# A mixture-of-experts tail on one Trainium2 core: the last expert's rows are placed by one-hot products on TensorE, and the other experts' rows are gathered and summed inside the round loop

## The reference

```python
top_v, top_i = lax.top_k(logits, TOP_K)          # TOP_K = 2 of N_EXPERTS = 8
gates = jax.nn.softmax(top_v, axis=-1)
combine = jnp.sum(jax.nn.one_hot(top_i, N_EXPERTS) * gates[..., None], axis=-2)
out = jnp.zeros_like(hn)
for e in range(N_EXPERTS):
    out = out + combine[..., e:e + 1] * swiglu(hn, w_gu[e], w_down[e])   # D_FF_EXPERT = 1024
return h + out
```

## Time and profile before

| | before |
|---|---|
| median of 3 runs | 1511.39 us (1510.7, 1511.39, 1518.9) |
| the profiled execution's own time | 1512.38 us |
| its span | 1510.7 us |
| PE busy | 1421.7 us (94%) |
| DVE busy | 898.5 us (59%) |
| ACT busy | 640.0 us (42%) |
| POOL busy | 241.2 us (16%) |

### The profile page before, as it was taken

How to read it: one execution, slowest core, us unless ns; L and a number is a source line. 1 busy time by engine, 2 the same in 40 slices (tenths; PEclk the granted TensorE clock), 3 DMA queues, 4 the chain that set the end, 5 groups by cost and what they waited for, 6 DMA issues and landing times. The chain is left out here.

```text
span 1510.7 us, 31344 instructions
## 1 busy us (share of the span) xinstructions
PE 1421.7 (94%) x12965; PEld 1263.5 (84%) x12965; DVE 898.5 (59%) x1201; ACT 640.0 (42%) x1077; POOL 241.2 (16%) x243
## 2 busy tenths in 40 slices
PE   6999999999899999999999998879799999999993
PEld 6999988888699999999999998549667777777772
DVE  5677635765755444434444666553467777777775
ACT  4344535442333223222323432563555656565561
POOL 0111016765120000000111101340042000000002
PEclk8999999999999999999999999799889999999997
DMA  6677422000433333332333522005269888888886
GB/s 186 222 280 265 135 66 63 2 2 30 151 116 84 97 98 83 85 109 58 96 91 116 168 57 91 1 1 150 76 210 303 297 279 296 292 276 285 272 286 219
DMA packets 170203, 226.48 MB, mean 150 GB/s; under 512 B 11545, under 2 KB 135090, under 8 KB 170010
## 3 DMA queue, kind: packets, MB, share of 16 engines
q1 hardware_dynamic: 160246, 191.44, 40.6%
q0 software_dynamic: 8976, 30.88, 5.8%
q10 hardware_dynamic: 862, 2.50, 0.5%
HBM read 188.78 MB, written 38.28 MB: 150 GB/s over the span
## 5 line engine op out<-in xcount | busy, mean ns | idle before, releaser
L281 DVE TENSOR_TENSOR w_lo<-w_raw,w_hi 128x2048 fp32r<-128x2048 f32 (+1 forms) x70 | 151.6, 2171 | 95.8 <-ACT w_hi L273 95.8
L226 PE MATMUL P<-xf_hi,w_hi 128*128 128x260 f32 x704 | 199.0, 283 | 2.0 <-DVEq L1857 1.2
L226 PE MATMUL P<-xf_hi,w_lo 128*128 128x260 f32 x704 | 198.9, 283 | 0.0
L226 PE MATMUL P<-xf_lo,w_hi 128*128 128x260 f32 x704 | 198.2, 282 | 0.0
L273 ACT ACTIVATE w_hi<-w_raw 128x2048 fp32r<-128x2048 f32 (+1 forms) x71 | 128.1, 1810 | 126.6 <-PE P L226 114.5
L226 PE MATMUL P<-xa_hi,w_hi 128*128 128x260 f32 x512 | 145.4, 284 | 5.0 <-DVE xa_lo L324 5.0
L226 PE MATMUL P<-xa_hi,w_lo 128*128 128x260 f32 x512 | 145.2, 284 | 0.0
L226 PE MATMUL P<-xa_lo,w_hi 128*128 128x260 f32 x512 | 144.8, 283 | 0.0
L226 PEld LDWEIGHTS P<-xf_hi,w_hi 128*128 128x128 f32 x704 | 132.5, 188 | 2.6 <-issue 1.4
L226 PEld LDWEIGHTS P<-xf_hi,w_lo 128*128 128x128 f32 x704 | 132.4, 188 | 0.0
L226 PEld LDWEIGHTS P<-xf_lo,w_hi 128*128 128x128 f32 x704 | 132.4, 188 | 0.0
(11 more groups left out here) (569 smaller groups left out, 3420.4 us busy)
## 6 DMA issues: line engine op xcount, KB each, us to landing
raw_more_moe<-in_moe_w_gu_dram SPq DMA_DIRECT2D x64, 512.0 KB, 5.3
w_raw<-in_moe_w_gu_dram SPq DMA_DIRECT2D x64, 512.0 KB
w_raw<-in_dense_w_gu_dram SPq DMA_DIRECT2D x44, 512.0 KB, 5.0
expert_out<-zeros POOLq DMA_DIRECT2D x40, 512.0 KB, 4.1
w_raw<-in_a_w_in_dram SPq DMA_DIRECT2D x32, 512.0 KB, 5.0
raw_more_moe<-in_moe_w_down_dram SPq DMA_DIRECT2D x32, 512.0 KB, 4.5
w_raw<-in_moe_w_down_dram SPq DMA_DIRECT2D x32, 512.0 KB
w_raw<-in_dense_w_down_dram SPq DMA_DIRECT2D x16, 384.0 KB, 4.0
```

What stands on the lines that cost most here:

```text
L226: ins = nc.tensor.matmul(out[:, b], w, x[:, b * HALF:(b + 1) * HALF], start=(first and n == 0), stop=(last and n == 2))
L281: ins = nc.vector.tensor_tensor(lo, raw, hi.bitcast(F32), ALU.subtract)
```

## The change

Expert 7's results are no longer stored to DRAM. TensorE's last two chunks are ordered by PSUM bank (`last_pair`), so that the over slots and the first half are complete early; ScalarE and VectorE split the results into high and low parts in SBUF (the over slots in a block-diagonal layout, which is cleared by two memsets first). TensorE then multiplies them by one-hot matrices (`spread_base`, `spread_over`), whose columns are tokens, so that PSUM holds expert 7's rows at the tokens' places: eight products of 128x512 per block of tokens, 40 in all. The one-hot matrices are made from expert 7's slot numbers, which GpSimd writes to a small DRAM table and reads back to all partitions, behind `read_table` and ahead of the gathers of tokens for experts 2 to 7. `hi_row` is now the highest slot among experts 0 to 6, `lo_row` the other one; both gathers read stored rows of experts 0 to 6 only (a near row whose expert is 7 has weight zero). The near gathers wait for experts 0 to 5, the far ones for expert 6. The gate weights are worked out in the loop in gate(3), the one-hots in gate(2), the near rows are added in down(6), and the far rows and the placed rows are added and stored at the end of the round. What follows the loop in the kernel before (the twelve small instructions and both additions) is gone.

```diff
+    spread_base, spread_over = flat_pick(1), flat_pick(0)
...
+    last_y_hi, last_y_lo = (xg[part][1].rearrange("p k s -> p (k s)") for part in range(2))
...
     wide = lambda bank: c.P[:, bank:bank + 2]
...
-                store_y(NE - 1)
-                for done, n in ((y_stored[0], 320), (y_stored[1], 240), (y_last, 80)):
+                for n, rows in blocks:
+                    sp.wait_ge(summed, r * NB + (n + 1))
+                    sp.sem_inc(passed, 1)
+                    to = io["y_prompt"][0, n * 128:(n + 1) * 128] if n < NCH else io["y_sample"].rearrange("b s d -> (b s) d")
+                    sp.dma_start(to, L.h_tok[0:rows, n]).then_inc(stored, 16)
+                for done, n in ((y_stored[0], 320), (y_stored[1], 240), (stored, 16 * NB)):
                     sp.wait_ge(done, r * n + n)
                     sp.sem_inc(passed, 1)
                 load_bound(sp, bound)
-            for n, rows in blocks:
-                sp.wait_ge(out_ready, n + 1)
-                to = io["y_prompt"][0, n * 128:(n + 1) * 128] if n < NCH else io["y_sample"].rearrange("b s d -> (b s) d")
-                sp.dma_start(to, L.h_tok[0:rows, n]).then_inc(stored, 16)
...
+                pool.wait_ge(rel_now, r + 1)
+                pool.sem_inc(passed, 1)
+                pool.dma_start(rel_table.rearrange("o (n p) -> p (o n)", p=128), rel[:, :, NE - 1],
+                               allow_slow_non_contiguous=True).then_inc(rel_out, 16)
+                pool.wait_ge(rel_out, r * 16 + 16)
+                pool.sem_inc(passed, 1)
+                pool.dma_start(rel_rows, rel_table.broadcast_to([128, NB * 128])).then_inc(rel_in, 16)
                 for e in range(2, NE):
...
-                for done, n in ((y_stored[0], 320), (y_stored[1], 240)):
-                    pool.wait_ge(done, r * n + n)
+                for done, n, past_ones in ((y_stored[0], 320, 240), (y_stored[1], 240, 240)):
+                    pool.wait_ge(done, r * n + past_ones)
                     pool.sem_inc(passed, 1)
                 for n, rows in blocks:
                     gather_y(near[n], L.lo_row, n, rows, near_in)
-                pool.wait_ge(y_last, r * 80 + 80)
+                pool.wait_ge(y_stored[0], r * 320 + 320)
                 pool.sem_inc(passed, 1)
                 for n, rows in blocks:
                     gather_y(far[n], L.hi_row, n, rows, far_in[n])
...
+                def last_pair(bank, over, hi, lo, fo):
+
+                    pair = (KT - 2, KT - 1)
+                    for t in pair:
+                        m = w.at["down", NE - 1, t]
+                        pe.wait_ge(w.lo_done, r * w.n + (m + 1))
+                        for b in range(4):
+                            ins = pe.matmul(c.P[b * OVER:(b + 1) * OVER, over, 0:256], fo[:, t % 2, t // 2 * OVER:(t // 2 + 1) * OVER],
+                                            w.raw[m % 8][:, b * 256:(b + 1) * 256], start=False, stop=(t == KT - 1))
+                    ins.then_inc(last_over, 1)
+                    for b in range(2):
...
+                            w_hi, w_lo = w.hi[m % 6], w.lo[m % 6]
+                            for a, x in ((hi, w_hi), (hi, w_lo), (lo, w_hi)):
...
+                        if b == 0:
+                            ins.then_inc(last_bank, 1)
...
+                def place_over(n, rows):
+
+                    for b in range(2):
+                        at = slice(b * 512, (b + 1) * 512)
+                        for y, done in ((last_over_hi, over_hi_done), (last_over_lo, over_lo_done)):
+                            if n == 0:
+                                pe.wait_ge(done, r * 4 + 4)
+                            pe.matmul(c.P[0:rows, place_bank[n] + b], spread_over[:, n * 128:n * 128 + rows], y[:, at],
+                                      start=(y is last_over_hi), stop=False)
+
+                def place_base(n, rows):
+
+                    for b in range(2):
+                        at = slice(b * 512, (b + 1) * 512)
+                        for y, done in ((last_y_hi, last_hi), (last_y_lo, last_lo)):
+                            if n == 0:
+                                pe.wait_ge(done, r * 2 + (b + 1))
+                            ins = pe.matmul(c.P[0:rows, place_bank[n] + b], spread_base[:, n * 128:n * 128 + rows], y[:, at],
+                                            start=False, stop=(y is last_y_lo))
...
-                    for _ in down(NE - 1, p, 2, 6, xg_hi[0], xg_lo[0], L.xo[:, 0].rearrange("p k s -> p (k s)")
-                                  .rearrange("p (u s) -> p u s", u=2)):
+                last = (2, 6, xg_hi[0], xg_lo[0], L.xo[:, 0].rearrange("p k s -> p (k s)").rearrange("p (u s) -> p u s", u=2))
+                for p in range(3):
+                    for _ in down(NE - 1, p, *last):
                         pass
-                pe.wait_ge(y_act, r * NE + (NE - 1))
+                last_pair(*last)
...
+                pe.wait_ge(y_act, r * (NE - 1) + (NE - 1))
+                pe.wait_ge(y_dve, r * (NE - 1) + (NE - 1))
+                pe.wait_ge(spread_done, r + 1)
                 pe.sem_inc(passed, 1)
+                place_over(0, 128)
+                place_over(1, 128)
+                place_base(0, 128)
+                place_base(1, 128)
+                for n in range(2, NB):
+                    if n == NCH:
+                        pe.wait_ge(summed, r * NB + 1)
+                        pe.sem_inc(passed, 1)
+                    place_over(n, blocks[n][1])
+                    place_base(n, blocks[n][1])
                 index(0, 5, r * 2 + 3)
                 load_bound(pe, bound)
...
-                        if e < NE - 1:
-                            nc.scalar.activation(y_rows[e % 2][:, 0:512], c.P[:, 4], ACT.Copy).then_inc(y_act, 1)
-                        else:
-                            nc.scalar.activation(flat2(y_rows[e % 2][:, 0:D]), wide(2), ACT.Copy)
-                            nc.scalar.activation(y_rows[e % 2][:, D:D + 256], c.P[:, 6, 0:256], ACT.Copy).then_inc(y_act, 1)
+                        nc.scalar.activation(y_rows[e % 2][:, 0:512], c.P[:, 4], ACT.Copy).then_inc(y_act, 1)
+                    if kind == "down" and q == KT - 1 and e == NE - 1:
+                        act.wait_ge(over_cleared, r + 1)
+                        act.wait_ge(last_over, r + 1)
+                        for b in range(4):
...
+                        act.wait_ge(last_bank, r + 1)
+                        nc.scalar.activation(last_y_hi[:, 0:512], c.P[:, 2], ACT.Copy).then_inc(last_hi, 1)
...
             pick(0)
-            stt(kept, chosen, -float(FAR), slots, ALU.mult, ALU.add)
-            reduce(lo_slot, kept, ALU.min)
-            reduce(hi_slot, tmp, ALU.max)
+            tt(kept, chosen, slots, ALU.mult)
+            reduce(lo_slot, kept, ALU.add)
+            reduce(hi_slot, tmp[:, :, 0:NE - 1], ALU.max)
...
+                def gates():
+
+                    count = 0
+                    def step(ins):
+                        nonlocal count
+                        count += 1
+                        ins.then_inc(gate_step, 1)
+                        dve.wait_ge(gate_step, r * GATE_STEPS + count)
+                    two_in = lambda to, a, b, op: step(nc.vector.tensor_tensor(to, a, b, op))
+                    dve.wait_ge(g_exp, 1)
+                    step(nc.vector.tensor_scalar(m1, g2, 1.0, None, ALU.add))
+                    step(nc.vector.reciprocal(m1, m1))
...
+                    step(nc.vector.tensor_reduce(g_hi, cand, AX, ALU.add))
+                    step(nc.vector.tensor_scalar(is_last, left, 1.0, None, ALU.is_equal))
+                    step(nc.vector.tensor_scalar(g_lo, g_lo, is_last, None, ALU.mult))
+                    step(nc.vector.tensor_scalar(g_hi, g_hi, is_last, None, ALU.mult))
+                    assert count == GATE_STEPS
...
+                def spread():
+
+                    dve.wait_ge(rel_in, r * 16 + 16)
+                    nc.vector.tensor_scalar(spread_base, rel_rows[:, 0:NT], cols(c, CTOK, 1), None, ALU.is_equal)
+                    nc.vector.tensor_scalar(spread_over, rel_rows[:, 0:NT], cols(c, COVER, 1), None, ALU.is_equal)\
+                        .then_inc(spread_done, 1)
+
+                def add_near(n, rows):
+
+                    if n == 0:
+                        dve.wait_ge(near_in, r * (16 * NB) + 16 * NB)
+                    nc.vector.scalar_tensor_tensor(L.h_tok[0:rows, n], near[n][0:rows], g_lo[0:rows, n:n + 1], L.h_tok[0:rows, n],
+                                                   ALU.mult, ALU.add).then_inc(near_added, 1)
+
+                def add_far(n, rows):
+
+                    dve.wait_ge(far_in[n], r * 16 + 16)
+                    dve.wait_ge(near_added, r * NB + (n + 1))
+                    nc.vector.scalar_tensor_tensor(L.h_tok[0:rows, n], far[n], g_hi[0:rows, n:n + 1], L.h_tok[0:rows, n],
+                                                   ALU.mult, ALU.add).then_inc(far_added, 1)
+
```

(44 more changed lines are left out.)

83 lines of the change are left out of this document (50 added, 33 removed).

## The result

The changed kernel takes 1521.36 us (median of 20 runs, 1516.5 to 1526.8) against 1514.39 us for the kernel before (20 runs, 1510.7 to 1523.1): ratio 1.0040, 95% interval 1.0025 to 1.0054. It is slower by 4 to 8 us, where 1.7 us less was forecast and 1515 was the upper end. Of the 11.7 us between the forecast of 1509.7 and 1521.36, 3.0 are the kernel before itself: its median is 1514.39 in 20 runs, and the forecast was made against 1511.39 in three. The profiled execution has a span of 1518.6 us (own time 1520.45), 7.9 us more than the one before.

What follows compares the result with a forecast made beforehand. Experts' stage bound by TensorE, weight stream close behind; tail by a DRAM round trip. Tail gain 4.65 less charges 2.95 gives 1.7 us, taken off the median 1511.39: 1509.7 us; range 1504.5 to 1515, the forecast's own 1507 to 1512.

Steps and rivals of the forecast that it cites:

- What is taken away: After TensorE's last products: expert 7's DRAM trip, twelve small instructions and near additions (4.88 us for four) leave the tail.
- the tail: After TensorE's last products at 1487.16: span ends at 1506.05, 4.65 us gained, if that point is reached as early.
- block 0: First block of tokens placed by TensorE in the tail, at about 1491.85, after twelve products of 0.227 us each.
- The terms behind the last addition: End of the round: small instructions 0.35 us, `pick` 0.99, casts 1.98, reload and branch 0.67 to 0.76, closing 0.4; given as 4.3.
- the table: Two DMAs for slot numbers, one waited for, ahead of experts 2 and 3's gathers, delaying them 6.5 us; charge 0.3, bounds 0 to 1.
- Near gathers: 2.1 MB moved from the tail into up(7), where the DMA engines are 91% busy; TensorE charged 0.5 us.
- rival C: Near gathers take turns with the weights, TensorE stands 1.3 to 2.5 us more: 1511 to 1512.2 us; chance 0.13.
- Low part behind the near additions: In down(6), near additions push expert 7's `low_f` to 1471.0, TensorE needs it at 1470.9: 0.15 us, between 0 and 0.5.
- Gate steps: 15 chained steps in gate(3) delay a split of up(3); TensorE stands 2.0 us, bounds 1.3 and 2.4; largest charge.
- Charges of 2.95 us: Costs ahead of TensorE's last products: 2.0 gate weights, 0.15 `low_f`, 0.5 near gathers, 0.3 table of slot numbers.
- D: TensorE's clock falls while waiting for over parts in the tail: 2.7 to 7.3 us more, 1512.4 to 1517; chance 0.12.
- Rival B: Gate steps don't stop TensorE and gathers find room: 1506.7 us, or 1505.5 with expert 6's store on time; chance 0.20.

Runs made afterwards that it cites:

- five edits: Changed kernel with table on TensorE, gate steps and near gathers spread out, two near additions later, TensorE's waits before the last pair: 1504.87 against 1512.12 us, 0.9957.

## Why the prediction was wrong

- **What is taken away, and the tail: right in the main.** Placing at full clock (0.227 us per product), eight additions in a row at 1.2 us, `pick` and the casts last. 18.2 us against 18.9 forecast; the gain is 5.4 us, not 4.65. That block 0 came so near its forecast is the cancelling of early far rows and a late signal (above). The terms behind the last addition add up to 4.4 to 4.5 us in the prediction, not to 4.3; 4.1 were measured.
- **The step that failed is the table**: "They are used much later, but meet other chunks: 0 to 1, taken as 0.3." It measured 6.1 us. I had priced the lateness of the gathers behind it and not the write itself, in 640 pieces of 4 bytes, which held the DMA engines and with them the weights. The upper end of 1 us was set by nothing. The nearest row of before, the read of 4-byte pieces with 4.0 us to landing, is not used in it, and would have said too little: the write's wait was 9.3 to 12.4 us in eight profiles.
- **Near gathers: mis-sized**, 0.5 forecast, 1.4 measured (1.1 to 4.2 in other profiles). The DMA engines were shared as rival C has it, about half to the weights, but C's loss would have been 1.8 to 3.0 us in all.
- **Low part behind the near additions: mis-sized**, 0.15 forecast (0.5 at most), 1.4 measured. The prediction walked VectorE's queue from the splits of the kernel before; in the changed one the chunks behind the near gathers came late as well, and VectorE has no idle time from 1464 to 1488, where I had counted on some.
- **Gate steps: right in place and near in size**, 2.0 forecast (1.3 to 2.4), 1.5 measured. Other profiles have 1.2 to 5.3, and why they differ so much is open.
- Charges of 2.95 us became 10.4. Against the tail's 5.4 that is 5.0 us slower, which is most of the ratio's 6; the table's spread from profile to profile is wide enough for the rest, which is argued and not shown. It ended on the slower side, but by none of the rivals as written: D (the clock in the placing) did not happen; the clock fell in up(1) instead.
- Rival B, inserted work hidden, did not happen in the changed kernel. It took five edits: 0.9957 and 0.9951 of 1512 us are 6.5 and 7.4 us less, 0.9987 on the chip with late signals.

That the four losses add up and that each edit removes its own is shown by the steps. What makes TensorE's signals late is open.

## What to carry to other kernels

Price a small DMA by how it is cut up, and look at what shares the DMA engines with it, not at who reads its result. Work moved out of a tail into a full stage was free here only when it was spread, one small instruction per chunk and one gather per few chunks, and did not stand ahead of what the critical engine waits for next. Pacing one thing can delay another that is queued behind it (1.0068), so edits of this kind are tried together as well as alone.

## What the runs showed of the hardware

- GpSimd waited 9.3 to 12.4 us, in eight profiles, for a write of 640 pieces of 4 bytes while weights were streaming, with 32 GB/s moved in its second half; for five pieces of 512 bytes 3.9. A read of 3.0 KB in 4-byte pieces landed in 4.0 us.
- TensorE's signals can arrive 1 to 6 us behind the end of the product in its record. Such signals are in the profiles of two sets and of the first two kernels, each time while GpSimd issues indirect DMAs (near 1112 to 1122, 1445 and in the tail: 2.1 us in the changed kernel's, at ScalarE's `remote` row above); ten profiles of three other sets show none, or one. The two sets ran on one chip and the three on three others, so it goes by the chip. On that chip three of the four kernels with the burst of near gathers have signals 1.7 to 4.2 us late near 1445, and the two with paced gathers have none there, which speaks for a part of GpSimd's DMAs in it. The cause is open.
- The five small products that spread the table, 2.5 us of work where TensorE otherwise idled for 1.5, had a side effect: its clock was at its upper level (2.4 GHz) when gate(0) began, at the lower one (1.2 GHz) in the kernel before, and TensorE's lag shrinks by 1.5 us over two chunks. Every profile of a kernel with these products has it, none of the others. The kernel with all edits, and the kernel before, over the stretch with gate(0):

```profile
1101.00:1125.00 24.00, 23.55 (x175) 16.92 (x176) 16.28 (x18) 12.98 (x15) 14.05 (x12) 1.00 0.77 242
```

```profile
1101.00:1125.00 24.00, 23.53 (x166) 16.73 (x166) 15.08 (x17) 12.51 (x14) 13.96 (x12) 0.92 0.68 224
```
